# Turning the input on the host and applying the norm's root after the projections

## The chip, the cores and the metric

The kernel runs on one core of one Trainium2 chip. The metric is the device time of one execution in microseconds, as the median of a few runs. Times inside the execution are counted from the start of the profiled span.

## The reference, cut to what matters

One decoder layer for 512 tokens of width 1024, all in float32:

```python
def hybrid_layer(x, ...):
    hn = rms_norm(x, g_pre_mix)            # x * rsqrt(mean(x*x) + eps) * g
    proj = hn @ w_in
    mq, mk, mv, fq, fk, fv, f_logit, cvb, cvc, cvh = jnp.split(proj, SPLIT_IDX, axis=-1)
    moba = moba_attention(heads(mq, 6), heads(mk, 6), heads(mv, 6), rel_bias)
    log_f = jax.nn.log_sigmoid((f_logit + b_f).astype(jnp.float32)).transpose(0, 2, 1)
    fox = forgetting_attention(heads(fq, 6), heads(fk, 6), heads(fv, 6), log_f)
    conv = cvb * causal_depthwise_conv3(cvc * cvh)
    mixed = jnp.concatenate([merge(moba), merge(fox), conv], axis=-1) @ w_out
    x = x + rms_norm(mixed, g_post_mix)
    h2 = rms_norm(x, g_pre_ffn)
    ff = (jax.nn.silu(h2 @ w_gate) * (h2 @ w_up)) @ w_down
    return x + rms_norm(ff, g_post_ffn)
```

With 512 tokens and blocks of 256, MoBA attends to everything causal, with a relative bias per head. The root factor of `rms_norm` is one number per token, so it can be multiplied into `hn` or into the rows of `hn @ w_in`; each of cvb, cvc and cvh carries it once.

## The kernel before, in words

Every float32 product is made of three TensorE products of rounded parts. An operand is split into a rounded high part (a copy by ScalarE, for the value weights by GpSimd) and the rest (a subtraction by VectorE): high times high, high times rest, rest times high. `product` (L1663) issues the three; a projection of 128 columns by 512 tokens is 8 steps (`proj_step`, one per 128 of the width), so 24 products of 512 columns.

**The opening (0 to 42.6 us).** The four token tiles of x come in by tokens. Per tile ScalarE squares and sums (`squares_of`), VectorE makes the reciprocal root and writes x times root times norm weight (`normalise`, L1120), the norm weight having been spread over the partitions by two TensorE products (`norm_weights`, L1677). TensorE turns the tile (`turn`, L1694), and ScalarE and VectorE split the turned tile into `hn_hi` and `hn_lo` (`tokens_hi`, `tokens_lo`). Then come the value projections of the three MoBA head pairs and the forget logits (390 columns, token tile by token tile, `v_rounded`, `v_token_rests`, `v_weight_rests`), 24 products a tile in one of the two banks `PROJ`; a small product for the relative bias (`relative_rows`); and the projections of q and k of the first pair of heads, `group(0, 0)` and `group(0, 1)`.

**The steps (42.6 to 192 us).** 48 attention steps follow, 8 for each of six pairs of heads. Step g takes one head and one tile of 128 queries. On TensorE it is written out as: logits of g (`logits_step`), three projection steps of the next pair as filler, in steps 2 and 6 of a pair the product of probabilities and values (`pv`), and then the turning of the probabilities of g-2 (`transpose_step`). VectorE adds the bias (`logits` written, `neg_max`), takes the rest of the turned probabilities of g-3 (`pT_lo`), and divides by the row sum. ScalarE takes the exponential of g and the high part of the turned probabilities of g-2 (`pT_hi`). The order on each engine is the order of the code; semaphores between engines count finished instructions. The six steps of a MoBA head use growing query tiles, those of the forgetting heads shrinking ones.

The q and k projections of the next pair end in steps 2 and 5 of a pair. ScalarE takes their high part from the bank with two copies (`evac_hi`, L790), VectorE the rest with two subtractions (`evac_lo`, L1191); the rest of k is due before the first logits of the next pair (`pe.wait_ge(proj_read, group(p, 1) + 1)` in `logits_step`). `conv_tail` works on the convolution's projections in the last pair. After the steps come the output projection, the norms and the feed-forward part, which are not touched.

## Time and profile before

| | |
|---|---|
| median of 3 runs | 575.78 us (575.10 to 575.89) |
| profiled execution, its own time | 576.57 us |
| its span | 574.8 us |
| first attention logits start at | 42.61 us |
| last attention logits start at | 188.98 us |
| TensorE busy | 567.5 us of the span |
| VectorE busy | 471.5 us |
| ScalarE busy | 319.7 us |

A row of a timeline gives the start, the length, the engine, the line of the kernel, the operation with what it writes and reads, and how many instructions were merged into the row; in brackets stands idle time of that engine before the row and what ended it. The length of a row runs to the end of its last instruction; instructions on one engine overlap at their ends, so a chain is read from start to start. A matmul's row also covers time in which it waited.

### The profile page before, as it was taken

To read this page: it belongs to the slowest core of one execution; us is meant where nothing else is said; L and a number is where in the kernel's file an instruction comes from. 1 tells how busy PE (TensorE), PEld (TensorE's weight loads), DVE (VectorE), ACT (ScalarE), POOL (GpSimd) and SP (SyncE) were. 2 spreads that over 40 slices of the span, in tenths; PEclk is the share of its full clock that TensorE was granted. 3 is DMA by queue.
4 is the path that set the end of the run, shared out by engine and by line. 5 is a ranking of instruction groups with operands and counts; after the bars stand their busy time and mean duration, and the time that the engine had idled before them with its cause. 6 is when DMAs were issued, how large, how long until landed. Compare 5 with 4: busy or idle time off the path is not lost.

```text
span 574.8 us, 9664 instructions
## 1 busy us (share of the span) xinstructions
PE 567.5 (99%) x3372; PEld 502.8 (87%) x3372; DVE 471.5 (82%) x791; ACT 319.7 (56%) x539; POOL 110.4 (19%) x129
## 2 busy tenths in 40 slices
PE   8999999999999999999999999999999999999996
PEld 6988888888888888899999999999999988888884
DVE  5647888888797954799888988988898788888787
ACT  5625765766555645575545546454554565547762
POOL 3020001103220000000324242332324002233100
PEclk9999999999999999999999999999999999999999
DMA  8274334346312471302323223242322359999743
GB/s 331 85 214 136 91 105 132 95 141 185 110 48 100 147 299 68 111 38 75 144 76 131 88 75 144 73 145 74 144 75 81 138 188 268 269 211 199 167 146 146
DMA packets 23144, 78.92 MB, mean 137 GB/s; under 512 B 2972, under 2 KB 2972, under 8 KB 23114
## 3 DMA queue, kind: packets, MB, share of 16 engines
q1 hardware_dynamic: 16716, 57.44, 28.2%
q0 software_dynamic: 6304, 21.00, 16.1%
q8 instruction: 17, 0.28, 0.2%
q10 hardware_dynamic: 94, 0.09, 0.0%
q14 instruction: 13, 0.11, 0.0%
HBM read 71.16 MB, written 4.22 MB: 131 GB/s over the span
## 4 chain that ended last, share of the span: by engine, by line
PE 99%; DVE 0%; POOL 0%; issue 0%; DVEq 0%; ACT 0%; POOLq 0%
PE bank L1666 11%; PE bank L1668 11%; PE bank L1667 11%; PE bank L1951 8%; PE bank L1950 8%; PE bank L1949 8%; PE bank L1957 7%; PE bank L2019 6%; PE bank L2017 6%; PE bank L2015 6%; PE bank L1960 3%; PE bank L1720 3%; PE bank L1827 3%; PE bank L1815 2%; PE bank L1805 1%; PE bank L1803 1%
## 5 line engine op out<-in xcount | busy, mean ns | idle before, releaser
L1950 PE MATMUL bank<-tok_lo,form_hi 128*128 128x256 f32 x320 | 90.6, 283 | 0.0
L1951 PE MATMUL bank<-tok_hi,form_lo 128*128 128x256 f32 x320 | 90.6, 283 | 0.0
L1949 PE MATMUL bank<-tok_hi,form_hi 128*128 128x256 f32 x320 | 90.5, 283 | 0.0
L1666 PE MATMUL bank<-hn,w_hi 128*128 128x512 f32 (+1 forms) x200 | 76.6, 383 | 0.0
L1668 PE MATMUL bank<-hn,w_lo 128*128 128x512 f32 (+1 forms) x200 | 75.0, 375 | 0.0
L1667 PE MATMUL bank<-hn,w_hi 128*128 128x512 f32 (+1 forms) x200 | 74.6, 373 | 0.0
L1949 PEld LDWEIGHTS bank<-tok_hi,form_hi 128*128 128x128 f32 x320 | 60.9, 190 | 1.9
L1951 PEld LDWEIGHTS bank<-tok_hi,form_lo 128*128 128x128 f32 x320 | 61.1, 191 | 0.0
L1950 PEld LDWEIGHTS bank<-tok_lo,form_hi 128*128 128x128 f32 x320 | 61.0, 191 | 0.0
L2015 PE MATMUL bank<-dw_hi,da_hi 128*128 128x512 f32 x154 | 59.9, 389 | 0.0
L2019 PE MATMUL bank<-dw_hi,da_lo 128*128 128x512 f32 x154 | 59.9, 389 | 0.0
L2017 PE MATMUL bank<-dw_lo,da_hi 128*128 128x512 f32 x154 | 59.9, 389 | 0.0
L1957 PE MATMUL bank<-hn,form_hi 128*128 128x512 f32 x160 | 58.1, 397 | 0.0
L712 POOL TENSOR_TENSOR sum_f<-raw 128x512 f32<-128x512 f32 x18 | 27.8, 1544 | 144.9 <-DVE form_lo L1457 144.9
L1457 DVE TENSOR_TENSOR form_lo<-sum_f,form_hi 128x1024 fp32r<-128x1024 f32 x40 | 48.6, 1216 | 0.0
L1457 DVE TENSOR_TENSOR form_lo<-raw,form_hi 128x1024 fp32r<-128x1024 f32 (+1 forms) x40 | 47.0, 1175 | 0.6
L859 ACT ACTIVATE probs<-logits,neg_max 128x128 f32<-128x128 f32 (+3 forms) x48 | 27.1, 564 | 36.4 <-DVE neg_max L1297 36.4
L971 ACT CAST form_hi<-sum_f 128x1024 fp32r<-128x1024 f32 x40 | 42.0, 1053 | 6.2 <-DVE sum_f L1395 5.9
L1960 PE MATMUL bank<-hn,form_lo 128*128 128x256 f32 x160 | 44.9, 281 | 0.0
L1668 PEld LDWEIGHTS bank<-hn,w_lo 128*128 128x128 f32 x200 | 37.7, 188 | 7.2
L1666 PEld LDWEIGHTS bank<-hn,w_hi 128*128 128x128 f32 x200 | 37.7, 189 | 6.1 <-issue 0.9
L1667 PEld LDWEIGHTS bank<-hn,w_hi 128*128 128x128 f32 x200 | 37.8, 189 | 5.1
(206 smaller groups left out, 1397.0 us busy)
## 6 DMA issues: line engine op xcount, KB each, us to landing
raw<-in_w_gate_units SPq DMA_DIRECT2D x22, 512.0 KB, 3.6
raw<-in_w_up_units SPq DMA_DIRECT2D x22, 512.0 KB, 4.5
raw<-in_w_in_units SPq DMA_DIRECT2D x21, 512.0 KB, 3.3
down_x<-in_w_down POOLq DMA_DIRECT2D x15, 512.0 KB, 9.7
down_y<-in_w_down SPq DMA_DIRECT2D x10, 512.0 KB, 9.2
raw<-in_w_out SPq DMA_DIRECT2D x8, 512.0 KB, 3.2
q_lh<-q_hl POOLq DMA_DIRECT2D x12, 256.0 KB, 2.8
down_x<-in_w_down SPq DMA_DIRECT2D x5, 512.0 KB, 3.9
```

What stands on the lines that cost most here:

```text
L1457: nc.vector.tensor_tensor(form_lo[par][:, sl, :, :], src, form_hi[par][:, sl, :, :], ALU.subtract).then_inc(form_lo_done, 1)
L1666: nc.tensor.matmul(out_ap, sh, mh, start=first, stop=False)
L1667: nc.tensor.matmul(out_ap, sh, ml, start=False, stop=False)
L1668: return nc.tensor.matmul(out_ap, sl, mh, start=False, stop=last)
L1949: nc.tensor.matmul(out_ap, sh, mh, start=first and k == 0, stop=False, skip_group_check=True)
L1950: nc.tensor.matmul(out_ap, sh, ml, start=False, stop=False, skip_group_check=True)
L1951: mm = nc.tensor.matmul(out_ap, sl, mh, start=False, stop=k == HK - 1, skip_group_check=True)
L1957: nc.tensor.matmul(bank[:, bank_no, :], form_hi[par][:, form, k, :], h2_hl[:, k0 + k, 0, :, :].rearrange("p two n -> p (two n)"), start=fi ...
L1960: mm = nc.tensor.matmul(bank[:, bank_no, 0:HALF], form_lo[par][:, form, k, :], h2_hl[:, k0 + k, 0, 0, :], start=False, stop=k == HK - 1, s ...
L2015: nc.tensor.matmul(out_ap, sh[:, k, tokens_of], mh[:, j, :], start=first and DOWN_CHAIN[n][1], stop=False, skip_group_check=True)
L2017: nc.tensor.matmul(out_ap, sh[:, k, tokens_of], ml[:, j, :], start=False, stop=False, skip_group_check=True)
L2019: return nc.tensor.matmul(out_ap, sl[:, k, tokens_of], mh[:, j, :], start=False, stop=last, skip_group_check=True)
```

## The change

x is handed over a second time, turned (`x_t`, the width on the partitions), and the norm weight as one number per partition (`g_feat`). `hn_hi` and `hn_lo` become the parts of x times norm weight, without the root, made directly from the loaded chunks; `normalise`, `norm_weights` and `turn` go. The values are projected width block by width block for all four token tiles, into four banks (4 to 7); the rests of the last chunk's weights come after q and k of the first pair. x by tokens is loaded later and gives the roots: ScalarE squares as before, VectorE spreads each root over 128 columns (`r_tok`), TensorE turns that (`row_scales`), ScalarE copies it to `r_open`, GpSimd to `r_cols`: the root of each token along the columns, on every partition.

The root is applied to results: value tiles by a per-partition scale in their two evacuations; the forgetting heads' values by a multiplication in place of a copy; q and k by a new VectorE multiplication from the bank into `qk_t` (`scaled_qk`), from which ScalarE and VectorE then take the high part and the rest; cvb and cvc times cvh by `r_cols2` (the root squared) in place of a copy, and one new multiplication of `conv_y` by `r_cols`. On ScalarE the high part of q or k now stands behind `pT_hi` of the same step.

```diff
-V_GROUPS = (0, 1, 2, 5)
+V_GROUPS = (2, 3, 4, 5)
-V_CHUNKS = ((0, 2), (2, 5), (5, 8))
+V_CHUNKS = ((0, 1), (1, 4), (4, 8))
+X_CHUNKS = ((0, 1), (1, 2), (2, 4), (4, 8))
+LATE_CHUNK = 2
...
+            def load_turned(n):
+                c = slice(*X_CHUNKS[n])
+                sp.dma_start(xt[:, c, :], x_t[:, c, :]).then_inc(xt_in[n], 16)
+
+            load_turned(0)
             load_values(0)
+            load_turned(1)
             load_values(1)
+            load_turned(2)
             load_values(2)
-            load_open(2)
-            load_open(3)
+            load_turned(3)
             load(3, unit(w_in_units, 0))
+            for t in range(TT):
+                load_open(t)
...
+            def tokens_hi(k):
+
+                chunk = next(n for n, (k0, k1) in enumerate(X_CHUNKS) if k0 <= k < k1)
+                act_e.wait_ge(xt_in[chunk], 16)
+                nc.scalar.activation(hn_hi[:, k, :], xt[:, k, :], ACT.Copy, scale=g_feat[:, k:k + 1]
+                                     ).then_inc(hn_hi_done, 1)
...
-                act_e.wait_ge(proj_done, G + 1)
...
+                act_e.wait_ge(proj_read, G + 1)
...
-                    last = nc.scalar.activation(dst[0:DH, h, :], bank[DH * h:DH * (h + 1), PROJ[G % 2], :], ACT.Copy,
+                    last = nc.scalar.activation(dst[0:DH, h, :], qk_t[DH * h:DH * (h + 1), :], ACT.Copy,
...
+            for k in range(4):
+                tokens_hi(k)
             act_e.wait_ge(rel_done, 1)
...
+            for k in range(4, KT):
+                tokens_hi(k)
             split(3)
+            for t in range(TT):
+                squares_of(t)
...
-                if g >= 1:
-                    for G in finished(g - 1):
-                        evac_hi(G)
...
                 if g >= 2:
                     evac_pT(g - 2)
+                if g >= 1:
+                    for G in finished(g - 1):
+                        evac_hi(G)
...
+            def row_scales(t):
+
                 inverse_std(SQ1, t)
+                nc.vector.tensor_scalar(r_tok[:, t, :], r_tok[:, t, :], rstd[:, SQ1, t:t + 1], None, ALU.mult
+                                        ).then_inc(r_tok_done, 1)
+
+            def scaled_qk(G):
+
+                _, p, j = kind_of(G)
+                dve.wait_ge(proj_done, G + 1)
+                if 2 * p + j:
+
+                    dve.wait_ge(qk_lo_done, 2 * p + j)
...
+                nc.vector.tensor_tensor(qk_t[:, :], bank[:, PROJ[G % 2], :], (r_cols if p else r_open)[:, :], ALU.mult
+                                        ).then_inc(proj_read, 1)
...
+                    dve.wait_ge(conv_step, 4 * c + 4)
+                    nc.vector.tensor_tensor(conv_y[:, :], conv_y[:, :], r_cols[:, :], ALU.mult
+                                            ).then_inc(conv_scaled, 1)
...
+            for u in range(V_UNITS):
+                pe.wait_ge(wv_hi_done, u + 1)
+                for k in range(*V_CHUNKS[u]):
+                    pe.wait_ge(hn_hi_done, k + 1)
+                    for t in range(TT):
                         v_mm(t, k, hn_hi, wv_hi, k == 0, False)
+                    pe.wait_ge(hn_lo_done, k + 1)
+                    for t in range(TT):
+                        v_mm(t, k, hn_lo, wv_hi, False, False)
+                    if u < LATE_CHUNK:
+                        pe.wait_ge(lo_done, u + 1)
+                        for t in range(TT):
+                            v_mm(t, k, hn_hi, wv_lo, False, False)
+                if u == LATE_CHUNK - 1:
+                    relative_rows()
+            pe.wait_ge(rel_copied, 2)
+            for k in range(KT):
+                proj_step(group(0, 0), V_UNITS, k)
+                if k == 3:
+                    row_scales()
...
-                    pe.wait_ge(proj_read, group(p, 1) + 1)
+                    pe.wait_ge(qk_lo_done, 2 * p + 2)
```

ScalarE in steps 5 to 7 of the first pair, before (`probs` is the exponential, `k_hl_100` the high part of k of the second pair, `pT_hi` the high part of turned probabilities):

```order
L806 CAST pT_hi<-bank 128x4x128 [waits t_done]
L859 ACTIVATE probs_86,row_sum<-logits,neg_max 128x384 [waits t_done,biased]
L790 ACTIVATE k_hl_100<-bank 64x512 [waits proj_done]
L790 ACTIVATE k_hl_100<-bank 64x512
L806 CAST pT_hi<-bank 128x128 [waits pv_done,t_done]
L859 ACTIVATE probs_87,row_sum<-logits,neg_max 128x512 [waits t_done,biased]
```

The same place on ScalarE in the changed kernel (`k_hl_104` is the same tile):

```order
L829 CAST pT_hi<-bank 128x4x128 [waits t_done]
L881 ACTIVATE probs_86,row_sum<-logits,neg_max 128x384 [waits t_done,biased]
L829 CAST pT_hi<-bank 128x128 [waits pv_done,t_done]
L813 ACTIVATE k_hl_104<-qk_t 64x512 [waits proj_read]
L813 ACTIVATE k_hl_104<-qk_t 64x512
L881 ACTIVATE probs_87,row_sum<-logits,neg_max 128x512 [waits t_done,biased]
```

The two instructions for k moved behind the one `pT_hi`, which waits for `t_done`, the turning at the end of TensorE's step, and they wait for a VectorE result instead of TensorE's.

VectorE in steps 6 and 7 of the first pair in the changed kernel (before, the row that writes `qk_t` isn't there, and the two of `k_hl` read the bank):

```order
L1277 TENSOR_TENSOR pT_lo<-bank,pT_hi 128x4x128 [waits pT_hi_done]
L1171 TENSOR_TENSOR qk_t<-bank,r_cols 128x512 [waits r_cols_done,qk_lo_done,proj_done]
L1135 TENSOR_TENSOR w_lo_75<-raw_66,w_hi_71 128x1024 [waits hi_done]
L1246 TENSOR_SCALAR f_z<-bank,bf_c 6x512 [waits small_in,f_rows_done]
L1376 RECIPROCAL row_inv<-row_sum 128x1 [waits exp_done]
L1378 TENSOR_SCALAR probs_86<-probs_86,row_inv 128x384 [waits inv_done]
L1237 SCALAR_TENSOR_TENSOR k_hl_104<-qk_t,k_hl_104 64x512 [waits proj_hi]
L1237 SCALAR_TENSOR_TENSOR k_hl_104<-qk_t,k_hl_104 64x512
L1342 ISA logits,neg_max<-bank,bias 128x512 [waits exp_done,s_done]
```

The multiplication into `qk_t` came in ahead of the weights' rest, and the rest of k stands where it stood, ahead of the last step's bias.

ScalarE's opening in the changed kernel, from the first chunk of turned x to the roots' copy:

```order
L792 ACTIVATE hn<-xt,g_feat 128x512 [waits xt_in0,g_in,consts_done]
L792 ACTIVATE hn<-xt,g_feat 128x512 [waits xt_in1]
L792 ACTIVATE hn<-xt,g_feat 128x512 [waits xt_in2] x2
L855 COPY rel_row<-bank 6x512 [waits rel_done]
L856 COPY rel_row<-bank 6x128
L792 ACTIVATE hn<-xt,g_feat 128x512 [waits xt_in3] x4
L770 CAST w_hi_69<-raw_68 128x1024 [waits raw_in3]
L773 ACTIVATE squares,sumsq<-x_open 128x1024 [waits x_in0]
```

The squares moved from the front to behind the split of the first q weights, and the high parts of width blocks 4 to 7 stand behind the copies of the relative rows.

## Rows read from the trace of the kernel before

**Rows 1.** Page, part 1: busy time, share of the span, instructions.
```profile
PE 567.5 (99%) x3372; PEld 502.8 (87%) x3372; DVE 471.5 (82%) x791; ACT 319.7 (56%) x539; POOL 110.4 (19%) x129
```

**Rows 2.** Windows: length, busy time and instructions of each engine, granted clock, DMA share, GB/s.
```profile
8.00:10.00 2.00, 2.00 (x10) 1.62 (x9) 1.92 (x4) 1.17 (x2) 1.38 (x2) 1.00 1.01 405
...
152.00:172.00 20.00, 20.00 (x101) 16.26 (x100) 17.72 (x47) 11.52 (x26) 5.03 (x9) 1.00 0.22 56
```

**Rows 3.** Timeline of TensorE in the opening.
```profile
9.78 1.91 PE L1702 MATMUL bank<-ident,xn 128*128 128x128 f32 x8
11.34 3.24 PE L1720 MATMUL bank<-wv_hi,hn 128*128 128x390 f32 x13
14.42 0.88 PE L1720 MATMUL bank<-wv_lo,hn 128*128 128x390 f32 x4
...
16.85 0.39 PE L1688 MATMUL bank<-onehot_r,relb_hl 33*6 33x512 f32 x1
...
17.52 1.69 PE L1720 MATMUL bank<-wv_hi,hn 128*128 128x390 f32 x8
...
27.30 0.47 PE L1666 MATMUL bank<-hn,w_hi 128*128 128x512 f32 x1
...
38.30 3.04 PE L1720 MATMUL bank<-wv_hi,hn 128*128 128x390 f32 x16
...
42.61 0.22 PE L1803 MATMUL bank<-k_hl,q_hl 128*128 128x128 f32 x1
```

**Rows 4.** Timeline of ScalarE in the opening.
```profile
4.22 1.06 ACT L752 ACTIVATE squares<-x_open 128x1024 f32<-128x1024 f32 x1 [0.78 <-DMA x_open<-in_x]
...
5.61 1.04 ACT L752 ACTIVATE squares<-x_open 128x1024 f32<-128x1024 f32 x1
...
17.63 0.58 ACT L835 COPY rel_row<-bank 6x512 f32<-6x512 f32 x1 [2.58 <-PE bank L1690]
...
33.06 1.20 ACT L790 ACTIVATE q_hl<-bank 64x512 fp32r<-64x512 f32 x2 [4.14 <-PE bank L1668]
```

**Rows 5.** Timeline of VectorE, the rest of q of the first pair.
```profile
34.29 1.40 DVE L1191 SCALAR_TENSOR_TENSOR q_hl<-bank,q_hl 64x512 fp32r<-64x512 f32 x2 [3.40 <-ACT q_hl L790]
```

**Rows 6.** Timeline of GpSimd in the opening: a rounding of value weights.
```profile
9.30 1.17 POOL L632 CAST wv_hi<-wv_raw 128x1170 fp32r<-128x1170 f32 x1 [0.62 <-DMA wv_raw<-in_w_v]
```

**Rows 7.** Timeline of TensorE: first logits of the second and of the sixth pair.
```profile
64.72 0.31 PE L1803 MATMUL bank<-k_hl,q_hl 128*128 128x128 f32 x1
...
162.79 0.48 PE L1803 MATMUL bank<-k_hl,q_hl 128*128 128x512 f32 x1
```

**Rows 8.** Timeline of ScalarE: last-but-one step of the first and of the fifth pair.
```profile
62.25 0.27 ACT L806 CAST pT_hi<-bank 128x128 fp32r<-128x128 f32 x1 [1.00 <-PE bank L1815]
...
160.44 0.59 ACT L806 CAST pT_hi<-bank 128x512 fp32r<-128x512 f32 x1 [0.52 <-PE bank L1815]
```

**Rows 9.** Timeline of VectorE: end of the second pair, then from the fifth to the sixth.
```profile
87.95 1.39 DVE L1191 SCALAR_TENSOR_TENSOR k_hl<-bank,k_hl 64x512 fp32r<-64x512 f32 x2
...
161.53 0.29 DVE L1297 CUSTOM_DVE_ANT_0 logits<-bank,bias 128x128 f32<-128x128 f32 x1
...
163.54 0.69 DVE L1297 CUSTOM_DVE_ANT_0 logits<-bank,bias 128x512 f32<-128x512 f32 x1 [0.66 <-PE bank L1805]
...
171.53 0.28 DVE L1231 TENSOR_TENSOR pT_lo<-bank,pT_hi 128x128 fp32r<-128x128 f32 x1
```

**Rows 10.** Timeline of TensorE: value product in the last pair's step 2.
```profile
171.16 0.39 PE L1666 MATMUL bank<-hn,w_hi 128*128 128x512 f32 x1
171.87 0.50 PE L1827 MATMUL bank<-pT_hi,v_fox 128*128 128x512 f32 x1
```

**Rows 11.** VectorE and ScalarE on 512 columns, from a bank and from memory.
```profile
66.77 0.68 DVE L1185 COPY vT<-bank 128x512 f32<-128x512 f32 x1
...
83.39 0.68 DVE L1246 TENSOR_TENSOR cat_lo<-o_sum,cat_hi 128x512 fp32r<-128x512 f32 x1
...
129.89 0.62 ACT L819 CAST cat_hi<-o_sum 128x512 fp32r<-128x512 f32 x1
```

More of the change, by code:

```diff
@@ L112, in group @@
 def group(p, j):
-    return 3 * p + 3 + j
+    return 3 * p + 3 + j if p else j
 def v_group(p):
@@ L348, in hybrid_block @@
         g_in = sem("g_in")
-        g_done = sem("g_done")
+        xt_in = [sem(f"xt_in{n}") for n in range(len(X_CHUNKS))]
+        ones_set = sem("ones_set")
+        r_tok_done = sem("r_tok_done")
+        r_turned = sem("r_turned")
+        r_open_done = sem("r_open_done")
+        r_cols_done = sem("r_cols_done")
+        r_cols2_done = sem("r_cols2_done")
+        qk_lo_done = sem("qk_lo_done")
+        conv_scaled = sem("conv_scaled")
         raw_in = [sem(f"raw_in{n}") for n in range(RAW)]
@@ L675, in _ @@
                 load_bias(p)
-                if p >= 1:
-                    swap(p)
+                swap(p)
+                if p == 0:
+                    pool.wait_ge(proj_done, V_GROUPS[-1] + 1)
+                    pool.wait_ge(r_open_done, 1)
+                    nc.gpsimd.tensor_copy(r_cols[:, :], r_open[:, :]).then_inc(r_cols_done, 1)
                 if p == 2:
@@ L1303, in _ @@
                 for G in finished(g - 1):
-                    if not has_hi(G):
+                    if has_hi(G):
+                        scaled_qk(G)
+                    else:
                         evac_lo(G)
@@ L1719, in v_mm @@
             def v_mm(t, k, part, weight, start, stop):
-                return nc.tensor.matmul(bank[:, PROJ[V_GROUPS[t] % 2], 0:V_COLS], part[:, k, P * t:P * (t + 1)],
-                                        weight[:, k, :], start=start, stop=stop)
-            def v_rounded(t, chunks=range(V_UNITS)):
-                for u in chunks:
-                    pe.wait_ge(wv_hi_done, u + 1)
-                    for k in range(*V_CHUNKS[u]):
-                        if k % 4 == 0:
-                            pe.wait_ge(hn_hi_done, 2 * t + k // 4 + 1)
-                        v_mm(t, k, hn_hi, wv_hi, k == 0, False)
```

234 lines of the change are left out of this document (91 added, 143 removed).

## The prediction

> **What bounds the kernel now.** I read the page's busy shares first, then windows of equal length, then the timelines of TensorE, ScalarE and VectorE beside each other in the opening and at the turns from one pair of heads to the next. TensorE is busy 99% of the span and VectorE 82% [rows 1]. A busy TensorE includes its waits, so the question is where its starts are further apart than its work. In the opening they are: from 9.78 to 11.34 us eight turnings of x take 1.56 us, and the thirteen 390-column products from 11.34 take 3.08 us, 0.24 each, against 4.31 us for 24, 0.18 each, from 38.30 on [rows 3]. The granted clock's column reads 1.00 in such a window [rows 2], but the durations tell of two levels: 390 columns in 0.325 us is 1.2 GHz, in 0.18 us 2.4 GHz with some overhead. If n of the thirteen ran at 0.325, 0.325n + 0.18(13-n) = 3.08 gives n = 5, so the clock rose near 13.0 us. From 27.30 to 38.30 the 48 products of q and k are dense, 0.229 each [rows 3]. In the steps between 42.61 and 189 us TensorE's starts are dense too: there anything later on VectorE or ScalarE costs nothing until a wait of TensorE is reached, and VectorE, 17.72 of 20 us busy in 152 to 172 [rows 2], has little room. So the change can gain only before 42.61 us, and can lose only at a few waits in the steps. The part after the steps is untouched and moves with TensorE.
>
> **The opening, rebuilt.** Gone are 32 turnings and two products that spread the norm weight; TensorE needn't wait for squares, roots and normalised tiles. What is left before the first logits is 96 products of 390 columns, the relative rows (16.85 to 17.52, 0.67 us), 48 products of 512 columns, and four new turnings of roots, which I price at 0.45 (the eight at the low clock took 0.195 each, half of that at the high one).
>
> The start: the windows move 405 GB/s when full [rows 2]; the first chunk of x and of the value weights together are 0.46 MB, against 0.52 MB of the first tile of x, which released the squares at 4.22 [rows 4]. I take the weights' chunk at 4.5, its rounding 0.45 (a third of 1.17 for 1170 columns, and some fixed part [rows 6]), so products from 5.1 us. The chunk of 1170 columns lies 1.4 MB into the stream, about 7.5 us, and is rounded by 8.8; the first twelve products at 0.325 end at 9.0, so this doesn't show.
>
> When the clock rises isn't in this trace for such a start. Bounds: in the trace it rose 1.7 us after the dense products began (11.34), which gives 6.8 us here, or at 13.0 whatever is done before. I take the middle, 10. Then by 10 us 15 of the first 48 products are done, the other 33 take 5.9, and the relative rows end at R = 16.6 (with 13, 18.0; with 6.8 the 1170-column chunk binds at 8.8 and its rest, 1.4 on VectorE, at 10.2, and R is 15.7).
>
> From R the chain is: ScalarE is queued at the relative rows, two copies (0.58 [rows 4], overlapping with a second, of a quarter of the columns: 0.73), then the high part of width block 4 at 0.55; TensorE idles 1.3 us. 32 products at 0.18: R+7.1. On VectorE four rests, the 1560-column rest and that of the first q weights are done at about R+7.2. ScalarE meanwhile: blocks to R+2.9, a split to R+3.9, four squares at 1.39 (4.22 to 5.61 [rows 4]) to R+9.4, roots spread at R+9.95, just when TensorE (twelve products of 0.229 further) asks for them. Projection of q ends R+13.2, of k R+18.7, the sixteen late products R+21.55. k's hand-over ends later: multiplication 0.69, ScalarE's pair 1.20 [rows 4], VectorE's pair 1.40 [rows 5], handovers 0.1, so R+22.1. First logits at 38.7 instead of 42.61: 3.9 us gained, between 2.5 (clock at 13) and 4.8 (clock early). Behind k's rest VectorE has four value tiles of about 0.85 each, so the first bias is 3.5 us after the first logits, where TensorE has 18 products of 0.229 and two logits, over 4.5 us, before the third logits ask for it: hidden.
>
> A late g_feat would move the start. Its 128 rows are 32 bytes each, issued first on ScalarE's queue. The Trainium skill (DMA: Bandwidth & Descriptors, "Latency and other measured facts") puts the fixed cost of a transfer at about 2 us whatever its size. By that it is there before x; no row shows one of this shape, and the sum has nothing for it.
>
> **The steps, what the new hand-over costs.** Per pair q and k each get one VectorE multiplication of 0.68 (as the copy that writes vT [rows 11]; rows overlap the next by some 0.08, so a queue counts 0.6). The copies that become multiplications (vT, conv_c) stay at 0.68 by the same row and that of cat_lo. The bank is freed earlier, which nobody waited for. For q the new order is hidden: its rest was done three steps before it is needed, and ScalarE's turned-probability copy stood right behind it anyway. For k it isn't. Before, ScalarE took k's high part in step 6 of a pair ahead of pT_hi; now it comes behind pT_hi, which starts at 62.25 in the first pair and at 160.44 in the fifth [rows 8]. From there:
> - first pair: 62.25 + 0.17 + 1.20 + 1.40 + handovers 0.1 = 65.15, where TensorE starts the next logits at 64.72 [rows 7]: 0.45 us of wait. The third pair is alike: 0.5.
> - second pair: VectorE is the later one. Its rest of k started at 87.95 [rows 9], straight behind other work, and the logits followed on its end; 0.6 more in that queue gives 0.6.
> - fourth and fifth pair (shrinking tiles: four blocks turned, pT_hi 0.59 long, and shorter next logits): 160.44 + 0.5 + 1.20 + 1.40 + 0.1 = 163.64 against 162.79 [rows 7]: 0.85 each.
> Sum over five turns: 3.25 us.
>
> Then the knock-on. In the fifth pair the bias of step 7, behind k's rest, starts at 163.65 instead of 161.53; VectorE's idle 0.66 before 163.54 [rows 9] swallows part, and with the exponential between, the sixth pair's first bias is 1.35 late against TensorE's 0.85. The new multiplication of conv_y adds 0.6 in the same queue. The rest pT_lo of 171.53 is what TensorE's value product at 171.87 waits for, and TensorE's own work ends at 171.16 + 3 x 0.229 = 171.85 [rows 9, 10]: no slack, so 0.5 + 0.6 = 1.1 us. By the same count the third turn leaves 0.15 at the next value product, the others nothing. Sum of the steps: 4.5 us (2.0 if the hand-overs run a third shorter and the knock-on is absorbed; 7 if every value product after a turn pays).
>
> The second conv multiplication falls in step 7 of the last pair, after which VectorE waits for a turning again: I price it at nothing, at most 0.6. GpSimd's new copy r_cols stands ahead of the second pair's bias and q swap, ten us before either is needed: nothing; moved ahead of its queue, at most 0.6.
>
> One rule bears on qk_t. From a bank to memory the rows show ScalarE at 0.59 for 512 columns [rows 8] and VectorE at 0.68; from memory ScalarE takes 0.62 and VectorE 0.68 [rows 11]: the turns get 0.06 longer at most. The Trainium skill (VectorE: DVE Perf Modes, "The TRN2 errata") gives VectorE a fixed part of 120 cycles from PSUM and 58 from SBUF, ScalarE 172 and 224. By the page k's pair on VectorE would be 0.13 us shorter and on ScalarE 0.09 longer, five turns 0.2 less in all; the rows show it for ScalarE and not for VectorE, so the sum stays as it is.
>
> **The sum.** 576.57 (the profiled execution's own time, of which 574.8 are span) - 3.9 + 4.5 = 577.2. That execution lies 0.8 above the median shown, so the forecast for the median is 576.4, rounded up for short restarts of TensorE behind each new wait to 576.5.
>
> **Rivals.**
> A (forecast). The opening's gain is given back at the turns. 576.5, with its own range 575.2 to 578.
> B. The gain stays. For: the steps' losses are each below 1 us and rest on starts that may shift once VectorE's work falls otherwise. Against: the order of ScalarE is fixed and pT_hi can't come before the turning. With 2.0 given back and 4.4 gained: 575.78 - 2.4 = 573.4.
> C, on the slow side: VectorE becomes the bound of the steps. Place: the rest pT_lo due before each value product in step 2 after a turn. Price: each of the five turns leaves VectorE 1 to 2 us behind, and 12% of idle repays that only over 8 us and more; it decides from the point where more than 1 us is left at step 2. At 0.8 more for each of four turns: 576.5 + 3.2 = 579.7. For: zero slack at 171.87. Against: idle like the 0.66 after the turns [rows 9].
> D. The opening doesn't get shorter as it says: the clock stays at 1.2 GHz until 13 us or later, and the roots' chain (squares behind the relative rows) holds q. Gain 1.5: 578.9.
>
> **How the numbers follow.** A 0.48, B 0.27, C 0.14, D 0.11. About 0.2% (1.15 us) is what a measurement of this kernel tells from no change; that is 574.6 to 576.9. A puts 0.63 within, 0.07 faster, 0.30 slower; B is faster in 0.85 of its cases, else within; C and D are slower, bar a tenth within. So faster 0.03 + 0.23 = 0.26, within 0.30 + 0.04 + 0.03 = 0.37, slower 0.37. Range 573.2 to 579.4: it takes in nearly all of A, about half of B, D, and some of C.
>
> **What would show it.** First logits near 38.7 and 390-column products at 0.18 from 10 us on; a TensorE gap of about 1.3 us right behind the relative rows. Waits of 0.4 to 0.9 before the first logits of pairs two to six, ended by VectorE's rest of k, and one near 1 us before the value product in the last pair's step 2. No such gaps, or first logits above 40, would prove the steps or the opening wrong; so would a gap at other value products (C).

## The result, and the profile after

The changed kernel is slower: 581.63 us (median, 580.53 to 582.1) against 575.67 us, a ratio of 1.0097 with a 95% interval of 1.0085 to 1.011. Its profiled execution took 582.1 us, of which 580.4 are span; before it was 576.57 and 574.8. One later execution of the kernel before, in the slow state (695 us at a mean clock of 0.755), is left out everywhere. The forecast was 576.5 with a range of 573.2 to 579.4: the measured median lies 5.1 us above the forecast and 2.2 above the top of the range.

The span falls into three parts, cut at TensorE's first logits (start of pair one) and at its 48th (last step):

| | first logits | first to last logits | behind the last | span |
|---|---|---|---|---|
| before | 42.61 | 146.37 | 385.82 | 574.8 |
| after | 41.59 | 152.17 | 386.64 | 580.4 |
| difference | -1.02 | +5.80 | +0.82 | +5.6 |
| predicted | -3.9 | +4.5 | 0 | +0.6 |

Each part came out longer than predicted. First the opening, TensorE's timeline of the changed kernel (columns as in [rows 3]: start, length, engine, line, operation, output<-input, shapes, count, and in brackets the idle time before it with what ended it):

```profile
5.48 1.96 PE L1753 MATMUL bank<-wv_hi,hn 128*128 128x390 f32 x8 [0.27 <-POOL wv_hi L652]
...
9.85 1.70 PE L1753 MATMUL bank<-wv_hi,hn 128*128 128x390 f32 x8 [1.69 <-POOL wv_hi L652]
...
17.43 0.22 PE L1728 MATMUL bank<-onehot_r,relb_hl 33*6 33x128 f32 x1
19.18 7.50 PE L1753 MATMUL bank<-wv_hi,hn 128*128 128x390 f32 x32 [1.54 <-ACT hn L792]
...
37.91 3.02 PE L1753 MATMUL bank<-wv_lo,hn 128*128 128x390 f32 x16
41.59 0.33 PE L1804 MATMUL bank<-k_hl,q_hl 128*128 128x128 f32 x1 [0.66 <-DVE k_hl L1237]
```

There are two idle stretches of TensorE, 1.69 and 1.54 us, where the kernel before had none of that size in front of its products. Behind the second the 32 products take from 19.18 to 26.52, 7.34 us, where 32 at 0.18 are 5.76. The windows of the same kernel (busy time of PE, PEld, DVE, ACT, POOL, then the granted clock, the DMA share and GB/s) show why:

```profile
18.00:20.00 2.00, 0.82 (x4) 0.79 (x5) 0.93 (x2) 2.00 (x5) 0.71 (x1) 0.94 1.03 410
20.00:22.00 2.00, 2.00 (x8) 2.00 (x7) 2.00 (x4) 2.00 (x4) 0.00 (x0) 0.50 0.90 335
22.00:24.00 2.00, 2.00 (x9) 2.00 (x9) 2.00 (x2) 1.97 (x4) 0.17 (x1) 0.71 0.09 37
```

The granted clock is 0.50, that is 1.2 GHz, for 3.4 us (from 19.75 to 23.16 by the trace's clock record), though TensorE had worked at 2.4 GHz since 6.1 us. In that stretch the products start 0.325 us apart, which is 390 columns at 1.2 GHz; before and after it they start 0.18 apart. The first idle stretch is the value weights' second chunk; GpSimd rounds it as soon as it lands, and it landed at 8.6 us, where the prediction has 7.5:

```profile
8.64 1.16 POOL L652 CAST wv_hi<-wv_raw 128x1170 fp32r<-128x1170 f32 x1 [3.21 <-DMA wv_raw<-in_w_v]
```

In the steps, the waits of TensorE's weight loads (columns: who waited for whom, us in total, times, longest):

```profile
PEld bank L1828 <- DVE pT_lo L1277: 4.9, 7, 1.6
PEld bank L1804 <- DVE k_hl L1237: 4.3, 6, 1.0
...
PEld bank L1713 <- DVE ext_lo L1135: 0.8, 1, 0.8
```

In the kernel before, the first of these was this, and of the second and third there was none:

```profile
PEld bank L1827 <- DVE pT_lo L1231: 1.4, 4, 0.4
```

The second row is the turns from one pair of heads to the next (a pair has eight steps, four for each head), with the wait before the first pair's logits. From the eighth logits of a pair to the first of the next it takes 3.18, 3.39, 3.26, 3.51 and 3.51 us, before 2.75, 2.81, 2.75, 2.63 and 2.63; 3.28 us more in all. The fifth turn as rows of ScalarE, VectorE and TensorE, beside [rows 7 to 9]:

```profile
163.02 0.59 ACT L829 CAST pT_hi<-bank 128x512 fp32r<-128x512 f32 x1 [1.61 <-PE bank L1816]
163.50 1.27 ACT L813 ACTIVATE k_hl<-qk_t 64x512 fp32r<-64x512 f32 x2
```

```profile
164.81 1.39 DVE L1237 SCALAR_TENSOR_TENSOR k_hl<-qk_t,k_hl 64x512 fp32r<-64x512 f32 x2 [1.56 <-ACT k_hl L813]
```

```profile
166.25 0.50 PE L1804 MATMUL bank<-k_hl,q_hl 128*128 128x512 f32 x1 [0.64 <-DVE k_hl L1237]
```

ScalarE idles 1.61 us for the turning of the probabilities, while the input of its work for k (`qk_t`, written by 161.58) is ready; then VectorE idles 1.56 us for ScalarE, then TensorE for VectorE. The first row of the waits is value products (`pv`). From the distances between logits, those of steps 10, 26, 30 and 42 (counting all 48 from 0) cost 0.74, 0.32, 0.54 and 1.28 us more than before, 2.88 together; the rest of the steps is 0.36 shorter in all. The third row stands behind the steps, in the output projection: it is the 0.8 of the last part.

### The profile page after: what moved, and what is told of

It is laid out like the page before. It is cut to its first block, busy times and chain, and to the rows that moved or that the text cites. A ratio compares the mean times of both kernels' runs of the same rounds, so it can differ in the third digit from the quotient of the medians.

```text
span 580.4 us, 9647 instructions
## 1 busy us (share of the span) xinstructions
PE 563.5 (97%) x3346; PEld 499.0 (86%) x3346; DVE 478.1 (82%) x809; ACT 322.2 (56%) x541; POOL 112.0 (19%) x131
## 3 DMA queue, kind: packets, MB, share of 16 engines
q0 software_dynamic: 6304, 21.00, 16.6%
## 4 chain that ended last, share of the span: by engine, by line
PE 83%; DVE 9%; issue 3%; ACT 2%; DMA 1%; POOL 1%; DVEq 0%; SPq 0%; ACTq 0%; POOLq 0%
PE bank L1952 8%; PE bank L1951 8%; PE bank L1950 8%; PE bank L1713 7%; PE bank L1715 7%; PE bank L1714 7%; PE bank L1958 6%; PE bank L2016 6%; PE bank L2020 6%; PE bank L2018 6%; PE bank L1961 3%; PE bank L1753 2%; PE bank L1828 2%; PE bank L1816 1%; ACT k_hl L813 1%
```

## The experiments

All times are medians, with the same split of the profiled span as above. The kernel before had medians of 575.74 to 576.17 beside them. "Changed" is the kernel of the diff. Each of best, best_k1 and best_mask also has the edits of the row above it; the others differ from the changed kernel by their own edit alone, and both is two of these together. A median and its profiled execution need not move alike: of the changed kernel's four executions three had the fall of the clock.

| | first logits | to the last | behind | span | median | ratio to before |
|---|---|---|---|---|---|---|
| changed | 41.59 | 152.17 | 386.64 | 580.4 | 581.63 | 1.0097 |
| rel_late | 38.21 | 152.22 | 386.57 | 577.0 | 578.83 | 1.0046 [1.0032, 1.0059] |
| fill | 39.30 | 152.27 | 386.63 | 578.2 | 580.29 | 1.0073 [1.0059, 1.0086] |
| fill_first | 40.30 | 152.13 | 386.97 | 579.4 | 581.73 | 1.0103 [1.0086, 1.012] |
| v1_early | 39.85 | 152.12 | 386.63 | 578.6 | 580.80 | 1.0085 [1.0071, 1.0098] |
| order_back | 39.11 | 148.86 | 386.53 | 574.5 | 577.37 | 1.0028 [1.0019, 1.0037] |
| no_qk | 41.59 | 147.76 | 386.55 | 575.9 | 576.25 | 1.0009 [0.9999, 1.0018] |
| conv_pool | 39.90 | 152.54 | 386.66 | 579.1 | 581.52 | 1.0097 [1.0083, 1.011] |
| no_convmul | 41.02 | 151.50 | 385.88 | 578.4 | 579.42 | 1.0055 [1.0041, 1.0069] |
| both | 38.69 | 148.83 | 386.58 | 574.1 | 575.37 | 0.9989 [0.998, 0.9998] |
| best | 37.97 | 148.20 | 385.93 | 572.1 | 574.03 | 0.9963 [0.995, 0.9977] |
| best_k1 | 37.57 | 147.86 | 385.87 | 571.3 | 573.19 | 0.995 [0.9936, 0.9963] |
| best_mask | 37.82 | 146.81 | 385.77 | 570.4 | 572.19 | 0.9936 [0.9922, 0.9949] |

### The idle behind the relative rows, and the clock

rel_late moves two copies on ScalarE (arguments cut):

```diff
-            act_e.wait_ge(rel_done, 1)
-            nc.scalar.copy(rel_row[:, 0:SEQ], ...)
-            nc.scalar.copy(rel_row[:, SEQ:REL], ...)
             for k in range(4, KT):
                 tokens_hi(k)
+            act_e.wait_ge(rel_done, 1)
+            nc.scalar.copy(rel_row[:, 0:SEQ], ...)
+            nc.scalar.copy(rel_row[:, SEQ:REL], ...)
```

> ScalarE copies the relative rows behind the high parts of width blocks 4 to 7, not ahead of them; nothing else changes. Theory (queue and clock): TensorE's idle of 1.54 us behind the relative rows goes, the granted clock of 0.50 in 20 to 22 us goes with it, and 32 products of 390 columns take 5.8 us instead of 7.34; together up to 3.1 us, of which the late second chunk's split may take back some: 578.3 to 579.6 against the changed kernel's 581.6. Rival (the data of block 4 is late, or the products of that stretch are slow for another reason, such as ScalarE and DMA traffic): less than 1 us gained, above 580.6.

578.83, 2.8 us below the changed kernel, in the range expected. The idle is gone and the 32 products follow at once, 0.18 us apart:

```profile
17.28 6.03 PE L1753 MATMUL bank<-wv_hi,hn 128*128 128x390 f32 x32
```

fill leaves the idle to the data, and gives TensorE something to do in it:

```diff
                 if u == LATE_CHUNK - 1:
                     relative_rows()
+                    for _ in range(14):
+                        nc.tensor.transpose(bank[:, R_BANK, 0:P], ident[:, :], ident[:, :])
```

> Fourteen turnings of the identity into an unused bank stand on TensorE behind the relative rows, in the 1.54 us in which it would wait; ScalarE's order stays. Theory (the idle lowers the clock): the wait stays as long as it was, the granted clock stays at 1.00 and the 32 products take 5.8 us instead of 7.34: 1.6 us gained, 580.0. Rival (those products are slow whatever TensorE did before): no gain, 581.6, and 0.325 us a product in 20 to 22 us again.

580.29, 1.3 us less than the changed kernel, with work that computes nothing. Its TensorE rows, then its windows:

```profile
16.64 1.75 PE L1772 MATMUL bank<-ident 128*128 128x128 f32 x14
18.24 6.00 PE L1753 MATMUL bank<-wv_hi,hn 128*128 128x390 f32 x32
```

```profile
20.00:22.00 2.00, 2.00 (x13) 2.00 (x12) 2.00 (x3) 1.97 (x4) 0.00 (x0) 1.00 0.82 300
```

The window touches thirteen products in place of eight, with ScalarE and DMA about as busy as before (1.97 against 2.00 us, 0.82 against 0.90). So the rival (contention) falls: the slow products were slow by the granted clock. Together the two runs split the 2.8 us into about 1.3 to 1.5 for the clock and the same for the idle. That the fourteen turnings kept the clock up is not shown by this run alone: the changed kernel's one execution without a fall took 580.53, and those of fill 579.89 to 580.76, and by the counts below five executions without a fall would come by chance about once in nine times.

The fall doesn't come in each execution. In the profile of order_back (below) the same idle of 1.54 us stands, and no fall follows:

```profile
8.65 1.70 PE L1753 MATMUL bank<-wv_hi,hn 128*128 128x390 f32 x8 [0.33 <-POOL wv_hi L652]
...
18.02 5.99 PE L1753 MATMUL bank<-wv_hi,hn 128*128 128x390 f32 x32 [1.54 <-ACT hn L792]
```

There the first idle stretch is short, so the next run, fill_first, filled that one, with the same fourteen turnings behind the products of chunk 0.

> Fourteen turnings of the identity stand on TensorE between the twelve products of the first chunk and the next, in the gap in which it waits for the second chunk; the idle of 1.54 us behind the relative rows stays. Theory (the fall of the clock near 20 us needs both gaps, as it came in the traces with 1.69 and 1.83 us of first gap and not in the one with 0.33): no execution has the clock of 0.994 to 0.996, the products from 18 us on take 0.18 each; the turnings themselves cost 0 to 1.2 us, so 580.5 to 581.7. Rival (the second idle alone does it, in a share of the executions): clocks 0.003 lower in a third or more of the runs, as in the changed kernel.

581.73, nothing gained; the median alone, at the upper end of the theory's range and beside the rival's, decides nothing, and one execution of 584.2 stays unexplained. But three of its six executions had a mean clock of 0.996, so the theory that both stretches are needed falls. Over all kernels that keep the idle behind the relative rows (the changed one, order_back, no_qk, conv_pool, v1_early, fill_first, no_convmul) 17 of 47 executions had 0.996 or less. Of those without it, none had: none of 31 in rel_late, both, best, best_k1 and best_mask, none of the 55 of the kernel before that ran beside them, and none of the 5 of fill. The 17 are a lower bound: the mean clock also takes in the end of the span, where it was low for 0.5 to 3.4 us in the fourteen traces, so that 0.997 can be either; order_back has one execution of 578.59 at 0.997. Of the seven profiles with the idle, the three with such a mean clock (0.996, 0.994, 0.995) show 0.50 in 20 to 22 us, the other four don't. So the idle behind the relative rows allows the fall; of the seven profiles without it (or with it filled) none shows one. What decides it in one execution stays open, but the traces hold a hint. The time at which the clock first rose differs between executions, and the three profiles with the fall have the earliest rises, at 5.9, 6.1 and 6.4 us; the four with the same idle and no fall have 6.6, 6.7, 7.9 and 8.2. The profile of fill has 8.5, so it would perhaps have had no fall in any case. Seven profiles prove no rule. Within a kernel the executions with a fall took 0.7 to 1.6 us more in the mean (1.3 in the changed kernel).

### The second chunk

v1_early asks for the value weights' second chunk ahead of the second block of x:

```diff
-            load_turned(1)
             load_values(1)
+            load_turned(1)
```

> The value weights' second chunk (585 KB) is asked for ahead of the second block of x (256 KB); the rest is the changed kernel. Theory (TensorE's gap of 0.3 to 1.8 us before its thirteenth product is the landing of this chunk behind 1.29 MB at 240 to 300 GB/s): the chunk lands 0.6 to 0.9 us earlier, the products behind it too, unless the second block of x or its high part is then the late one; 0.5 to 0.9 us gained, 580.7 to 581.1, and fewer executions in which the clock falls. Rival (the landing is set by something else, such as a queue's fixed latency or the roots' chain behind it): 581.6.

580.80, but its executions without a fall took 580.3 to 581.4 where the changed kernel's took 580.53: no gain that can be told apart. The chunk did land at 7.60, and the wait moved to the condition named: the second block of x came at 8.22, its high part at 8.9, and the products start at 9.09. A transfer pushed ahead of another that is wanted as soon only changes places with it here. best_k1, below, does it otherwise.

### The turns

order_back puts ScalarE's high part of q and k ahead of the turned probabilities again; VectorE keeps its multiplications.

```diff
+                if g >= 1:
+                    for G in finished(g - 1):
+                        evac_hi(G)
                 if MOBA_PAIRS <= p + 2 < PAIRS and s == 2:
...
                 if g >= 2:
                     evac_pT(g - 2)
-                if g >= 1:
-                    for G in finished(g - 1):
-                        evac_hi(G)
```

> In the steps ScalarE takes the high part of q and k ahead of the turned probabilities again, as in the kernel before; VectorE's multiplication stays. Theory (at the turns k's high part is late because it stands behind pT_hi on ScalarE): in the fourth and fifth pair it comes 1 to 2 us earlier and the turn's wait of 0.88 goes; in the first three VectorE's queue keeps some of it: 2 to 3.3 us gained, 578.3 to 579.6. Rival (VectorE's longer queue alone makes the turns late): 0.5 us or less, 581.1 or more.

577.37, a larger gain than expected, because most of its executions went without the clock's fall and most of the changed kernel's with it; with the fall it took 578.2 and 578.6, against 581.3 to 582.1. The steps alone went from 152.17 to 148.86, 3.31 us. The turns now take 2.85, 3.39, 2.75, 2.63 and 2.63: four are as before (the first within 0.1 here, within 0.2 in both and best), and the second pair's keeps its 0.58 through VectorE's queue, as expected of it. ScalarE of the fifth turn:

```profile
157.29 1.27 ACT L813 ACTIVATE k_hl<-qk_t 64x512 fp32r<-64x512 f32 x2 [0.20 <-DVE qk_t L1171]
158.70 0.59 ACT L829 CAST pT_hi<-bank 128x512 fp32r<-128x512 f32 x1
```

It waits 0.20 us for VectorE's product, and does k's part in the time in which it sat idle in the changed kernel. The value products of step 26 (3.97 again) and part of step 42 (5.54 to the next logits, 6.10 in the changed kernel, 4.82 before) went with it.

no_qk leaves out the multiplication of q and k in the steps, ten on VectorE, and has ScalarE's old order.

```diff
-                    if has_hi(G):
-                        scaled_qk(G)
-                    else:
+                    if not has_hi(G):
                         evac_lo(G)
```

> In the steps q and k are taken from their banks without the multiplication by the tokens' reciprocal roots, so ten multiplications of 0.68 us are left out on VectorE, and ScalarE's order is that of the kernel before; the opening, vT, conv_c and conv_y keep theirs. Theory (turns 3.3 us, and the waits of the value products in steps 10, 26 and 30, some 1.3 to 1.6 us, come from these multiplications): 576.7 to 577.3, turn gaps of 2.63 to 2.8 us, with the value product of step 42 0.6 to 0.7 late for the conv_y multiplication and 0.8 at the output projection left. Rival (the value products wait for something else of the change): 578.2 or more, with those waits still there.

576.25, a little below the range expected, because seven of its eleven executions went without the fall; with it, it took 577.5 to 577.8 (581.3 to 582.1 in the changed kernel). The steps take 147.76, 4.41 less than in the changed kernel and 1.10 less than in order_back: all turns are those of before, and steps 10 and 30 too (3.76 and 4.23 to the next logits). So those two waits come from the multiplications themselves. Left over are 0.72 in step 42 and 0.73 behind the steps. In the first pair it has a wait of 0.6 that the changed kernel doesn't: q's bank is free only after VectorE's rest of q (0.35 us of idle at 56.07 us), so the multiplication, which frees it earlier, pays back a little there.

### conv_y

conv_pool gives conv_y's multiplications to GpSimd: the first stands behind the last pair's first mask in its queue, the second behind all masks (line cut at its end).

```diff
-                    nc.vector.tensor_tensor(conv_y[:, :], conv_y[:, :], r_cols[:, :], ALU.mult
+                nc.gpsimd.tensor_tensor(conv_y[:, :], conv_y[:, :], r_cols[:, :], ALU.mult
```

> The multiplication of conv_y by the reciprocal roots (two of 0.69 us) is done by GpSimd between its masks, not by VectorE; all else is the changed kernel. Theory (each of the two stands whole on the path through VectorE): the value product of the last pair's step 2 comes 0.65 us earlier and the wait of 0.8 us for ext_lo in the output projection goes: 1.4 us gained, 580.2 against 581.6. Rival (they are covered, or GpSimd's copy makes the masks or VectorE late): within 0.4 us of the changed kernel.

581.52, no gain: the rival was right in its number, and the profile shows how. Rows of GpSimd, then of VectorE:

```profile
170.11 1.29 POOL L692 TENSOR_TENSOR conv_y<-conv_y,r_cols 128x512 f32<-128x512 f32 x1 [3.12 <-DVE conv_y L1204]
...
191.86 2.20 POOL L692 TENSOR_TENSOR conv_y<-conv_y,r_cols 128x512 f32<-128x512 f32 x1 [2.76 <-DVE conv_y L1204]
```

```profile
170.13 1.55 DVE L1384 TENSOR_SCALAR probs<-probs,row_inv 128x512 f32<-128x512 f32 x1
...
191.70 1.22 DVE L1144 TENSOR_TENSOR w_lo<-raw,w_hi 128x1024 fp32r<-128x1024 f32 x1
...
193.02 1.19 DVE L1384 TENSOR_SCALAR probs<-probs,row_inv 128x256 f32<-128x256 f32 x1
```

VectorE's scaling of the probabilities, started 0.02 us behind GpSimd's instruction, takes 1.55 us; the same form takes 0.49 elsewhere. In the second place VectorE's subtraction of two tiles started first and kept its 1.22, GpSimd's instruction was stretched to 2.20, and the scaling behind it took 1.19 and ended 0.15 behind GpSimd's, where 256 columns take 0.35. The Trainium skill (SBUF — State Buffer, "Who interferes with whom") says that VectorE and GpSimd share a pair of ports as an exclusive lock, and that of two instructions that need it the one issued first keeps it for its whole length; the rows shown agree with that. The two don't slow each other down by halves: the later one waits. Step 42 takes 6.40 us to the next logits here, 0.30 more than in the changed kernel.

So the price had to be found otherwise. no_convmul leaves the two multiplications out, so its convolution lacks one factor.

> The two multiplications of conv_y by the reciprocal roots are left out (so the convolution's output lacks one factor); all else is the changed kernel. Theory (both stand whole on the path, and GpSimd's version gave nothing because VectorE's scaling of the probabilities took 1.55 and 1.19 us instead of 0.49 and 0.36 while GpSimd multiplied): step 42's value product 0.6 to 0.7 us earlier, the output projection's wait of 0.8 gone: 1.3 to 1.5 us gained at the same clock, 579.1 to 580.6. Rival (covered work): within 0.4 us of the changed kernel.

579.42, 2.2 below the changed kernel. At like clocks the means differ by 1.4 to 1.7 (580.12 against 581.3 to 582.1 with the fall, 578.9 to 579.4 against 580.53 without). The steps are 0.67 shorter and the part behind them 0.76: both multiplications stood on the path with nearly all of their 0.69 us.

### Together

both is rel_late and order_back in one.

> The copies of the relative rows behind blocks 4 to 7 on ScalarE, and ScalarE's high part of q and k ahead of the turned probabilities. Theory (the two repairs are of different stretches and add up: 2.8 and, taken at the same clock, 3.4 to 3.7): 575.1 to 575.5, 0.6 to 1 us below the kernel before. Rival (with the steps starting at 38.2 instead of 39.1 to 41.6, the roots' chain or VectorE's late value tiles take a part back): 576 to 577.

575.37, as expected: the two add up, and the kernel is at last just below the one before. Its trace has a first idle of 1.20 us where rel_late's has 0.62, and its first logits are at 38.69 and not at 38.21.

best moves conv_y's two multiplications on VectorE to where it has time: the first behind the rest that step 42's value product waits for, the second into an idle of 0.50 us.

```diff
+                if g == STEPS:
+                    conv_scale(1)
                 if g >= 3:
                     evac_pT(g - 3)
...
                 else:
+                    if c == 0:
+                        conv_scale(c)
                     dve.wait_ge(conv_scaled, c + 1)
```

> Both repairs of before, and conv_y's multiplications moved on VectorE: the first behind the turned probabilities' rest of step 2 of the last pair, just before its result is used, the second into the idle of 0.50 us before the last but two of those rests. Theory (what counts is the place in VectorE's queue, not the work): step 42's value product 0.65 us earlier, 0.3 to 0.5 off the wait for ext_lo: 1 to 1.2 us below the 575.37 of both repairs, 574.2 to 574.4. Rival (another instruction of VectorE is late in its place): 575.0 or more.

574.03, 1.3 less with the same instructions, a little below the range expected. Step 42 takes 4.82 to the next logits, the number of before, and the wait for ext_lo is gone (385.93 behind the last logits): the place in the queue was the price, not the 0.69 us.

best_k1 splits the second chunk's transfer and rounding at its first block, and TensorE takes the twelve products with these weights' rests behind the others of the chunk (the transfers alone are shown):

```diff
-            load_values(1)
+            sp.dma_start(wv_raw[:, 1:2, :], w_v[:, 1:2, :]).then_inc(wv_one_in, 16)
+            sp.dma_start(wv_raw[:, 2:4, :], w_v[:, 2:4, :]).then_inc(raw_in[1], 16)
```

> The last one, and the value weights' block 1 comes in a transfer and a rounding of its own, with blocks 2 and 3 in a second; TensorE takes the twelve products with the weights' rests behind the others of the chunk. Theory (the gap before the thirteenth product is the landing of 585 KB in one piece): block 1 is rounded about 1.3 us before the whole chunk was, eight products move into the gap, the relative rows end 0.5 to 1.3 us earlier, and the first logits too unless the roots' chain (r_tok) is then late: 573.2 to 574.0. Rival (the roots bind at once, or a new idle lets the clock fall): 574.2 to 575.5.

573.19, at the lower end of the theory's range and 0.8 below best. The first block's rounding starts at 7.01 us:

```profile
7.01 0.51 POOL L656 CAST wv_hi<-wv_raw 128x390 fp32r<-128x390 f32 x1 [1.64 <-DMA wv_raw<-in_w_v]
7.97 0.84 POOL L658 CAST wv_hi<-wv_raw 128x780 fp32r<-128x780 f32 x1 [0.45 <-DMA wv_raw<-in_w_v]
```

The first logits moved by 0.4 only, because TensorE's wait moved on to the third block of x, whose high part starts at 9.95 when it lands:

```profile
10.82 3.08 PE L1771 MATMUL bank<-wv_hi,hn 128*128 128x390 f32 x16 [0.85 <-ACT hn L801]
```

The rest of the 0.8 has no place of its own: the same chunk's landing differs by up to 1.3 us between executions, and there is one trace.

The last run follows from step 30, the fourth pair's seventh. These are GpSimd and VectorE in the changed kernel, one step ahead of its value product (the bias is that of the pair's sixth step):

```profile
131.92 0.53 POOL L660 DMA_DIRECT2D q_lh<-q_hl  x1 [1.43 <-DVE q_hl L1237]
132.46 0.31 POOL L686 TENSOR_SCALAR_AFFINE_SELECT bias<-bias 128x128 f32<-128x128 f32 x1
```

```profile
132.94 0.56 DVE L1342 CUSTOM_DVE_ANT_0 logits<-bank,bias 128x384 f32<-128x384 f32 x1 [0.60 <-POOL bias L686]
```

and in the kernel before:

```profile
130.23 0.53 POOL L640 DMA_DIRECT2D q_lh<-q_hl  x1 [2.32 <-DVE q_hl L1191]
130.77 0.31 POOL L666 TENSOR_SCALAR_AFFINE_SELECT bias<-bias 128x128 f32<-128x128 f32 x1
```

GpSimd waits for VectorE's rest of q, issues the swap, and only then masks the bias that VectorE wants. The fourth logits of that pair stand at 125.12 and at 123.96, so the mask starts 7.34 us behind them where it was 6.81: q's multiplication, 0.53 later, all the way through. VectorE's idle of 0.60 for the mask is in the kernel before too (ahead of 131.25), so this order of GpSimd's queue probably cost there as well. best_mask moves the swap behind two masks:

```diff
-                if p + 1 < PAIRS:
-                    swap(p + 1)
-                for i in (2, 1, 0):
-                    mask(p, 1, i)
+                mask(p, 1, 2)
+                mask(p, 1, 1)
+                if p + 1 < PAIRS:
+                    swap(p + 1)
+                mask(p, 1, 0)
```

> The fastest so far (573.19), with GpSimd's two issues of the next pair's swapped q moved behind the masks of the second head's second and third tile; before they stood ahead of them, and the second waits for VectorE's rest of q. Theory (in the fourth pair the multiplication of q is not hidden: it delays q's rest, GpSimd's swap behind it, the mask behind that, the bias of step 5 and the value product of step 6, 0.5 us): the idle of 0.59 us of VectorE before that bias goes, the gap from the fourth pair's seventh to its eighth logits falls from 4.77 to 4.0 to 4.25, the rest stays: 572.4 to 572.8. Rival (VectorE's own queue makes the value product of that step late): 573.0 or more, gap 4.7 again.

572.19, a little better than expected. The bias comes without a wait, from the seventh to the eighth logits it takes 4.07 where it took 4.77 (4.24 in the kernel before), and the same place in the fifth pair gave another 0.3:

```profile
127.18 0.55 DVE L1359 CUSTOM_DVE_ANT_0 logits<-bank,bias 128x384 f32<-128x384 f32 x1
```

This kernel computes all that the changed one does and is 0.64% faster than the kernel before.

## Why the prediction was wrong

**The opening (3.9 us predicted, 1.02 measured).** Three terms failed. The first is "The chunk of 1170 columns lies 1.4 MB into the stream, about 7.5 us": it landed at 8.6. The only rate that the prediction names is that of a full window, 405 GB/s [rows 2]; in the windows up to the landing the changed kernel moves 255, 290 and 339 (last column):

```profile
2.00:4.00 2.00, 1.61 (x8) 1.62 (x9) 0.00 (x0) 1.28 (x1) 0.29 (x1) 1.00 0.93 255
4.00:6.00 2.00, 1.73 (x8) 1.33 (x7) 0.68 (x2) 0.72 (x1) 0.51 (x1) 1.00 0.88 290
6.00:8.00 2.00, 2.00 (x12) 1.83 (x10) 1.30 (x3) 0.72 (x1) 0.00 (x0) 1.00 1.02 339
```

The clock column says 1.00 in these windows, but it knows no level ahead of the first recorded change, at 6.1 us: TensorE's turnings from 2.39 us on start 0.213 us apart, where four at 29.3 us start 0.109 apart.

The relative rows end at 17.65, predicted 16.6: 1.05 us. The second term is "TensorE idles 1.3 us": it was 1.54, 0.24 more, 0.17 of it because ScalarE's copy with a pointer scale takes 0.72 us where the prediction has 0.55. The third is the "32 products at 0.18": the clock fell behind the very idle that the prediction forecast, and they took 7.34 us in place of 5.76: 1.58 us. The sum is 2.87, which is the miss. The prediction treats the clock as something that rises once.

That the first of these is only 1.05 us is partly luck. The 16.6 rests on a rise of the clock at 10 us, and it rose at 6.1. For an early rise the prediction has its own figure, 15.7 (its terms, 8.8 + 36 x 0.18 + 0.67, give 15.95), and against that the relative rows are 1.7 to 1.95 us late: the chunk is rounded at 9.8 and not at 8.8, TensorE waits again for the rest of its weights (0.19 us before 11.74), and each restart takes about 0.1. The late rise that the prediction put in covered 0.65 to 0.9 of this.

The chain from the relative rows on was right: with the idle and the fall out, in rel_late, the first logits come 20.9 us behind the relative rows' end, and R+22.1 less the idle of 1.3 is 20.8. Nor is the fall the whole miss: the changed kernel's one execution without it took 580.53, still 1.1 above the range.

g_feat landed at 4.49 us, 3.7 us from its issue, 0.89 after ScalarE was ready and 0.19 after the first chunk of x. The 2 us that I cited from the Trainium skill (DMA: Bandwidth & Descriptors, "Latency and other measured facts") for a transfer's fixed cost didn't hold beside a full stream, and neither did what the prediction concluded from it, that g_feat is there before x; the measurement decides. It cost nothing, since the weights' rounding ended later still.

**The turns (3.25 predicted, 3.28 measured).** Right in size, place and mechanism: turn by turn 0.45, 0.6, 0.5, 0.85 and 0.85 were predicted, and 0.43, 0.58, 0.51, 0.88 and 0.88 measured. order_back takes away all but the part that the prediction gave to VectorE's queue (0.6 for the second pair; 0.58 is left). The handed-over k costs about what the rows of before say: ScalarE's pair took 1.27 us from memory (1.20 for q from a bank), VectorE's 1.39 from either.

**The knock-on (1.25 predicted, 2.88 measured).** "0.5 + 0.6 = 1.1" for step 42 was 1.28: order_back takes 0.56 of it away, and no_convmul 0.73. "By the same count the third turn leaves 0.15": 0.32. But "the others nothing" failed twice. Step 10 cost 0.74, and it goes with the multiplications (no_qk) and not with the order (order_back). In the kernel before VectorE has no idle from 59.33 to 70.83 us in which 0.6 us more could be lost; the lateness reaches the value product through the exponentials and ScalarE's queue (VectorE waits 0.73 us for pT_hi ahead of 72.46). Step 30 cost 0.54, from "for q the new order is hidden": the prediction looked at who reads q, three steps later, and not at GpSimd's queue, where the swap waits for q's rest and the bias's mask stands behind it; best_mask shows this. Elsewhere the steps were 0.36 shorter, by two gains of 0.25 in steps 13 and 21 that also go with the multiplications; they were not followed up.

**Behind the steps (0 predicted, 0.82 measured).** "I price it at nothing, at most 0.6": the second conv_y multiplication is the 0.8, by no_convmul (0.76 gone). The wait "for a turning again" behind step 7 didn't take it up; best, which puts the multiplication into an idle of 0.50 us further on, gains 0.65 there.

**The rivals.** C had the right side and partly the right place: of the four late value products three (steps 10, 26 and 42) stand in a step 2 behind a turn, as it said. But they cost 0.74, 0.32 and 1.28, together 1.09 above the forecast's 1.25 and not 3.2, and the fourth (step 30) came by GpSimd's queue. D was nearest in the opening: it did fall short, and in part because of the clock, yet by a fall and not by a late rise, and the roots' chain held nothing (TensorE has no idle at the turnings of the roots at 29.27). Three parts erred to the same side, and no rival let the opening and the steps fail together. Of the costs priced at nothing, two (q's new order and the second conv_y multiplication) would have needed a look past the next reader of the result.

## What to carry to other kernels

A wait that you add can be paid by everything queued behind it on that engine, so follow each added wait through the queues of all engines, DMA issuers too, not only to the reader of its result. Where an instruction gets a new dependence, look for the place in its queue where the engine would idle anyway: here four such moves (the relative rows' copies, the high parts of q and k, conv_y's multiplications, GpSimd's swap) and one split transfer turned a loss of 1.0% into a gain of 0.6% with the same arithmetic. And an idle of TensorE in an otherwise dense stretch can cost twice: by its length, and by the clock behind it.

## What the runs showed that was not expected

- Behind an idle of 1.54 us the mean granted clock was 0.996 or less in 17 of 47 executions. In the three of them that were profiled it fell from 1.00 to 0.50 for 3.4 us, which cost 1.58 us in the changed kernel. None of 86 executions without the idle had so low a mean clock, nor any of five with fourteen turnings in it, which are too few to show that these prevent the fall.
- A GpSimd multiplication of 512 columns (1.29 us) held up VectorE's scaling that started 0.02 us behind it (0.49 became 1.55 us), so work moved off VectorE to GpSimd came back as a wait of VectorE.
- The same chunk of weights landed between 7.43 and 8.78 us in ten traces (by the start of GpSimd's rounding), with nothing changed in the transfers ahead of it.
